# Three edits to a one-core twelve-stage network kernel: what is loaded first, where retention's angle tables are made, and when the convolution asks for the rows of its norm's scale

## The reference, cut to what matters

```python
def rmsnorm(x, gain=None):                 # in front of every mixer and MLP
    y = x * lax.rsqrt(jnp.mean(x * x, axis=-1, keepdims=True) + NORM_EPS)
    return y * gain

def rotary(t, positions):                  # in retention, on q and k
    half = t.shape[-1] // 2
    inv_freq = ROPE_BASE ** (-jnp.arange(half) / half)
    ang = positions[:, None, :, None] * inv_freq
    cos, sin = jnp.cos(ang), jnp.sin(ang)
    t1, t2 = t[..., :half], t[..., half:]
    return jnp.concatenate([t1 * cos - t2 * sin, t2 * cos + t1 * sin], axis=-1)

def conformer_conv(u, w_in, b_in, w_dw, ...):
    a, gate = jnp.split(u @ w_in + b_in, 2, axis=-1)
    h = a * jax.nn.sigmoid(gate)           # then 31 taps along the sequence
    ...
```

## Time and profile before

| | |
|---|---|
| median of 3 runs | 2310.38 us (2308.9 to 2310.8) |
| the profiled execution | 2314.51 us, of which 2312.7 us are the span from its first to its last instruction |
| PE busy | 2223.2 us, 96% of the span |
| PEld, DVE, ACT, POOL busy | 81%, 65%, 52%, 10% |
| moved by DMA | 368.93 MB, 160 GB/s on average |
| mean granted TensorE clock | 0.984 of full speed |

### The profile page before, as it was taken

One profiled execution on the slowest core, in us unless ns is written; L12 is line 12 of the kernel. 1 busy time (PEld: TensorE's weight loads), 2 busy tenths in 40 slices (PEclk: granted clock), 3 DMA queues, 4 the chain that ended last, 5 costly groups with the idle time before them and its releaser, 6 DMA issues.

```text
span 2312.7 us, 29470 instructions
## 1 busy us (share of the span) xinstructions
PE 2223.2 (96%) x11634; PEld 1880.1 (81%) x11634; DVE 1493.3 (65%) x2081; ACT 1197.6 (52%) x1817; POOL 223.6 (10%) x204
## 2 busy tenths in 40 slices
PE   6999999999999999999999999977999999999999
PEld 5877888887888878888878888766888888798887
DVE  4745755896656767557745665785665798454665
ACT  4555544755445745445555544654544666455543
POOL 0000100472000011000000100001000000152000
PEclk9999999999999999999999999988999999899999
DMA  6535566523665535554544655423655666302553
GB/s 214 182 129 181 168 196 193 162 68 97 191 197 174 166 107 187 195 198 156 182 145 146 194 184 195 167 92 90 197 183 181 199 170 184 127 1 88 186 189 121
DMA packets 201528, 368.93 MB, mean 160 GB/s; under 512 B 6943, under 2 KB 142495, under 8 KB 201392
## 3 DMA queue, kind: packets, MB, share of 16 engines
q1 hardware_dynamic: 197776, 358.70, 47.7%
q0 software_dynamic: 3616, 8.35, 2.2%
HBM read 365.97 MB, written 1.05 MB: 159 GB/s over the span
## 4 chain that ended last, share of the span: by engine, by line
PE 86%; DVE 6%; ACT 5%; issue 1%; POOL 1%; DMA 1%; SPq 0%; DVEq 0%; ACTq 0%
PE PS L656 46%; PE PS L781 14%; PE PS L778 6%; PE PS L765 6%; ACT whi L1311 2%; PE PS L934 2%; PE PS L1255 2%; DVE wlo L1854 2%; PE PS L1224 1%; PE PS L855 1%; PE PS L798 1%; ACT side L1361 1%; PE PS L1026 1%; ACT U L1346 1%; PE PS L780 1%
## 5 line engine op out<-in xcount | busy, mean ns | idle before, releaser
L1854 DVE TENSOR_TENSOR wlo<-raw,whi 128x1024 fp32r<-128x1024 f32 x658 | 792.4, 1229 | 206.2 <-ACT whi L1311 205.3
L1311 ACT ACTIVATE whi<-raw 128x1024 fp32r<-128x1024 f32 x680 | 700.1, 1056 | 392.4 <-PE PS L656 321.5
L781 PE MATMUL PS<-U,whi 128*128 128x512 f32 x1440 | 508.6, 397 | 5.1 <-DVE wlo L1854 5.1
L656 PE MATMUL PS<-whi,U 128*128 128x512 f32 x1728 | 483.2, 396 | 9.6 <-DVE U L2295 3.4
L656 PEld LDWEIGHTS PS<-whi,U 128*128 128x128 f32 x1728 | 322.5, 189 | 83.8 <-issue 14.3
L778 PE MATMUL PS<-U,wlo 128*128 128x256 f32 x1260 | 353.5, 281 | 0.0
L781 PEld LDWEIGHTS PS<-U,whi 128*128 128x128 f32 x1440 | 264.7, 188 | 58.5 <-issue 6.8
L656 PE MATMUL PS<-wlo,U 128*128 128x512 f32 x864 | 268.3, 392 | 0.0
L1980 DVE TENSOR_TENSOR AR<-PS,AR 128x512 f32<-128x512 f32 x96 | 66.3, 691 | 309.0 <-ACT AR L1398 308.9
L656 PE MATMUL PS<-whi,fH 128*128 128x512 f32 x832 | 258.1, 391 | 0.9 <-DVE fL L2103 0.9
L656 PE MATMUL PS<-whi,fL 128*128 128x512 f32 x832 | 256.4, 389 | 0.0
(11 more groups left out here) (323 smaller groups left out, 2451.0 us busy)
## 6 DMA issues: line engine op xcount, KB each, us to landing
raw<-in_mlp_w_up SPq DMA_DIRECT2D x64, 1024.0 KB, 5.6
raw<-in_mlp_w_down SPq DMA_DIRECT2D x64, 1024.0 KB, 5.0
raw<-in_ret_w_in SPq DMA_DIRECT2D x48, 1024.0 KB, 5.2
raw<-in_m_w_up SPq DMA_DIRECT2D x32, 1024.0 KB, 5.6
raw<-in_m_w_down SPq DMA_DIRECT2D x32, 1024.0 KB, 5.0
raw<-in_kv_w SPq DMA_DIRECT2D x24, 1024.0 KB, 5.2
raw<-in_ret_w_out SPq DMA_DIRECT2D x16, 1024.0 KB, 4.9
raw<-in_gla_w_in SPq DMA_DIRECT2D x12, 1024.0 KB, 5.1
```

The source lines that it names most:

```text
L656: mm = e.matmul(bank(b + nb), a, w[:, nb * 512:(nb + 1) * 512], start=(begins and n < 2), stop=(ends and n >= 4))
L781: mm = e.matmul(o, w_h[:, k, :], U[:, k, :, :, :], start=(k == 0), stop=(k == 7))
L1311: e.activation(split_half(whi, i, x), a, ACT.Copy).then_inc(HI.tick((i, x)), 1)
L1854: e.tensor_tensor(split_half(wlo, i, x), a, split_half(whi, i, x).bitcast(F32), ALU.subtract).then_inc(LO.tick((i, x)), 1)
```

## The change

1. **SP** issues the identity, half tt 0 of x, chunk 0 and half tt 1 of x, then waits until chunk 0 has landed, and issues chunks 1 to 3. **POOL** issues gT, `invf`, `positions` and decay, waits for the same landing, and then issues `relP`, `relN` and the two rows of norm gains.
2. **`angles`** becomes a generator. In RET0 DVE runs all of it behind the low part of chunk 0. For RET1 it runs in MLP2, two steps behind each of the parts f = 2, 3, ... of the MLP. **`sines`** runs in MLP2 behind part f = 11, with a `prime()` behind it, and in RET0 behind the squares of h. At the very start ACT runs a `prime()`, and it makes the high part of chunk 1 before that of tt 1 of u.
3. **In CONV** PE asks for the rows of the scale in the middle of the second chunk (between its two halves), ACT makes the high part of the third chunk before it copies the rows, and DVE makes its low part before `scaled(0)`.

```diff
             def gemm_b(i, b, free=(), mid=None):
                 for s in range(2):
+                    if s == 1 and mid is not None:
+                        mid()
                     e.wait_ge(*lo_cut(i, s))
...
-                rows_of_r(S, p.dg, 3)
                 for c in range(1, 8):
-                    gemm_b(c0 + c, 5 + (c - 1) % 3, free=[CXX[c - 3]] if c >= 4 else [])
+                    gemm_b(c0 + c, 5 + (c - 1) % 3, free=[CXX[c - 3]] if c >= 4 else [],
+                           mid=(lambda: rows_of_r(S, p.dg, 3)) if c == 1 else None)
...
             def act_mlp(S):
...
                     e.activation(fH[:, f % 3, :], m_x[f % 2], ACT.Copy).then_inc(FH.tick((S, f)), 1)
+                    if f == 11 and S + 1 in RETS:
+                        sines(S + 1)
+                        prime()
...
             def act_conv(S):
                 p, c0 = PC, first[S]
+                hi_of(c0 + 1, 1)
                 e.wait_ge(*ROWR[S])
...
             e.wait_ge(*s_gT[1])
+            prime()
             next_in(RET0, 0)
-            hi_to(1)
+            hi_to(2)
             next_in(RET0, 1)
-            hi_to(2)
             squares(RET0)
+            sines(RET0)
             act_ret(RET0)
...
             def dve_mlp(S):
...
+                steps = angles(S + 1) if S + 1 in RETS else iter(())
                 for f in range(16):
...
+                    if f >= 2:
+                        next(steps, None)
+                        next(steps, None)
...
             def dve_ret(S):
...
-                lo_of(c0, 1)
-                angles()
-                lo_of(c0 + 1, 1)
                 rows_of_r(S, p.dg)
-                lo_of(c0 + 2, 1)
+                lo_of(c0, 3)
                 tables()
...
             def dve_conv(S):
...
-                lo_of(c0, 1)
+                lo_of(c0, 2)
                 for c in range(8):
...
             lo_to(1)
+            for _ in angles(RET0):
+                pass
             u_lo_next(RET0 - 1, 1, 0, 1, 2, 3)
...
             def pool_ret(S):
...
-                load(p.relP, d["rel"][0].rearrange("(a p) n -> p a n", p=128), par["rel"])
-                load(p.relN, d["rel"][1].rearrange("(a p) n -> p a n", p=128), par["rel"])
                 load(p.invf, d["invf"], par["inv"])
                 load(p.posi, d["positions"][0, :].partition_broadcast(128), par["pos"])
                 load(p.lg, ...)
+                if S == RET0:
+                    e.wait_ge(*landed(0))
+                load(p.relP, d["rel"][0].rearrange("(a p) n -> p a n", p=128), par["rel"])
+                load(p.relN, d["rel"][1].rearrange("(a p) n -> p a n", p=128), par["rel"])
...
             load(gT[:, :, :], d["gains_in"], s_gT)
+            pool_ret(RET0)
             load_gain(RET0)
             load_gain(MLP0)
-            pool_ret(RET0)
...
             e.dma_start(ident[:, :], d["ident"]).then_inc(s_id.sem, 16)
-            for i in range(NCH):
+            load_x(0)
+            load_chunk(0)
+            load_x(1)
+
+            e.wait_ge(*landed(0))
+            for i in range(1, NCH):
                 load_chunk(i)
```

More of the change, by code:

```diff
@@ L752, in fresh_u, with gemm_b @@
                 return lambda k, tt: [UL[t, tt, k // (2 if t[1] == "in" else 4)]]
-            def gemm_b(i, b, free=()):
+            def gemm_b(i, b, free=(), mid=None):
                 for s in range(2):
+                    if s == 1 and mid is not None:
+                        mid()
                     e.wait_ge(*lo_cut(i, s))
@@ L1407, in act_mlp, with sines @@
                     seam(S)
+            def sines(S):
+                p = PR
+                for w, dst, arg in (("cos", p.cos, p.kf), ("sin", p.sin, p.ang)):
+                    e.wait_ge(*ANG[S, w])
+                    e.activation(dst, arg, ACT.Sin).then_inc(SIN.tick((S, w)), 1)
             def act_ret(S):
@@ L1422, in raw @@
                     ins.then_inc(QKCP.tick((S, n)), 1)
[L1424 to L1427, removed]
                 def log_decay():
@@ L1987, in dve_mlp, with angles @@
                     e.tensor_tensor(fL[:, f % 3, :], x, fH[:, f % 3, :].bitcast(F32), ALU.subtract).then_inc(FL.tick((S, f)), 1)
+                    if f >= 2:
+                        next(steps, None)
+                        next(steps, None)
                 lo_to(first[S + 1])
                 seam(S)
+            def angles(S):
+                p = PR
+                ang, kf = p.ang, p.kf
+                e.wait_ge(*s_ret_par["pos"][RETN[S]])
+                own(e.tensor_copy(ang, p.posi))
+                yield
+                settle()
+                e.wait_ge(*s_ret_par["inv"][RETN[S]])
+                own(e.tensor_scalar(ang, ang, p.invf[:, 0:1], None, ALU.mult))
+                yield
+                settle()
+                own(e.tensor_scalar(kf, ang, float(1 / (2 * np.pi)), 12582912.0, ALU.mult, ALU.add))
+                yield
+                settle()
+                own(e.tensor_scalar(kf, kf, -12582912.0, None, ALU.add))
+                c1 = 6.28125
+                c2 = float(np.float32(round((2 * np.pi - c1) * 2 ** 21) / 2 ** 21))
+                c3 = float(np.float32(2 * np.pi - c1 - c2))
+                for cc in (c1, c2, c3):
+                    yield
+                    settle()
+                    own(e.scalar_tensor_tensor(ang, kf, -cc, ang, ALU.mult, ALU.add))
+                yield
+                settle()
+                own(e.tensor_scalar(kf, ang, float(np.pi / 2), None, ALU.is_gt))
+                yield
+                settle()
+                own(e.scalar_tensor_tensor(kf, kf, float(-2 * np.pi), ang, ALU.mult, ALU.add))
+                yield
+                settle()
+                own(e.tensor_scalar(kf, kf, float(np.pi / 2), -3.1415925, ALU.add, ALU.max))
+                yield
+                settle()
+                e.tensor_scalar(kf, kf, 3.1415925, None, ALU.min).then_inc(ANG.tick((S, "cos")), 1)
+                e.tensor_scalar(ang, ang, 3.1415925, -3.1415925, ALU.min, ALU.max).then_inc(ANG.tick((S, "sin")), 1)
             def dve_ret(S):
                 p, c0 = PR, first[S]
-                lt, lg, ang, kf = p.lt, p.lg, p.ang, p.kf
+                lt, lg = p.lt, p.lg
                 cosb = p.cos.unsqueeze(1).to_broadcast([128, 2, 256])
```

28 lines of the change are left out of this document (1 added, 27 removed).

## The result

The changed kernel takes **2295.72 us** (median of 4 runs, 2295.4 to 2296.52) against 2310.2 of the kernel before on the same chip (4 runs, 2308.9 to 2310.8): ratio 0.9939, 95% interval 0.9921 to 0.9956. That is 14.5 us less; the forecast was 2294.1, 16.3 less, with a range of 2289.5 to 2301.0. The interval of the ratio stands for a gain of 10.2 to 18.3 us. The profiled execution took 2296.52 with a span of 2294.7; a second one, of the same kernel, is told of under the experiments.

A forecast was written before the change was run, and what follows sets the result against it. The prediction took PE, with 86% of the chain of waits, to bound the kernel. Start and RET0 12.3, RET1 4.2 and CONV -0.2 made 16.3 us, from 2310.38 to 2294.1 us; range 2289.5 to 2301.

The forecast's parts named there:

- Chunk 0 lands at 9.3; ACT's chain ends last, at 10.1: Start: ACT's high part of u, not chunk 0's landing, ends last; PE starts at 12.3 instead of 19.92.
- Chunk 1 lands at 17.6, 0.6 too late: Start: chunk 1, issued at 9.3, takes 8.3 us though needed by 17.0, so PE restarts at 21.0.
- The risk itself: Start: chunk 1 comes late, at 24.7, and PE restarts at 28.1; gain 6.8, time 2303.6, chance 0.15.
- Restart 7.0 earlier: Start: PE's restart with half tt 1 comes at 21.0 instead of 28.01, gaining 7.0 us.
- The wait of 3.8 and a dip of 1.5 go in RET0: RET0: PE's wait for the rows and the slow-clock stretch behind it vanish, 3.8 and 1.5 us.
- Rival B: RET0 and RET1: slow-clock dips do not go with the waits but fall elsewhere; gain 13.3, time 2297.1, chance 0.11.
- RET1: 2.7 + 1.5 = 4.2: RET1: the diagonal is made earlier, so PE's wait of 2.7 us goes with the dip that follows.
- The block in MLP2 costs nothing, cover 2.2: MLP2: ACT's added 3.6 us of loads, sines and prime stay hidden, with 2.2 us of cover left.
- Rival D: MLP2: ACT's block or DVE's steps reach PE, a 0.6 stall with a dip; 2.1 less, time 2296.2, chance 0.05.
- CONV -0.2: CONV: PE's 1.6 wait goes, but it idles 4.7 instead of 3.0 before the first sum; worth -0.2.
- rival E: CONV: more POOL products meet DVE's subtraction, each costing 1.9 us; with 20 more, 2332 us; chance 0.02.
- The sum: Whole kernel: 12.3 + 4.2 - 0.2 = 16.3 us off the median 2310.38, giving 2294.1 us.

The follow-up runs named there:

- best: Changed kernel with ten of PE's CONV taps before the first sum, x's second half after the wait for chunk 0, prime() before ACT's wait for gT: 2300.97 us.
- best_u_first: best with ACT making u of half tt 1 ahead of chunk 1's high part: 2293.64 us, ratio 0.9928.
- the second trace of before: Second profile of the kernel before, unchanged, taken in before_again; its profiled execution was 4.6 us shorter than the first.
- loads_only: Kernel before with only the new order of SP's and POOL's loads: 2303.68 us, ratio 0.9972.
- fill_wait: Kernel before with 22 unread PE products in front of the rows of the scale in both retentions: 2306.63 us, ratio 0.9987.
- double_block: Changed kernel with ACT's block in MLP2 made 3.0 us longer by two more table loads with one-column activations: 2295.32 us, ratio 0.9935.
- no_conv_edit: Changed kernel with the edit in the convolution undone: 2294.73 us, ratio 0.9932.
- the second set: Runs of after_again, no_conv_edit, best and no_pool_wait, beside which the kernel before took 2310.7 us.
- before_again: Kernel before, unchanged, profiled a second time: 2310.02 us, ratio 1.0001.
- after: Changed kernel, first measurement and trace, against the kernel before: 2295.72 us, ratio 0.9939.
- after_again: Changed kernel, unchanged, run and profiled a second time: 2296.43 us, ratio 0.9937.
- conv_fill: Changed kernel with eleven of PE's taps of group 7 put in front of the first sum in CONV: 2293.55 us, ratio 0.9932.
- no_pool_wait: Changed kernel in which POOL does not wait for chunk 0 before issuing rel: 2299.24 us, ratio 0.9949.
- best_pool_late: best with POOL's loads of rel and the gains waiting for chunk 1 instead of chunk 0: 2293.68 us, ratio 0.9928.

## Why the prediction was right, step by step

- **Chunk 0 lands at 9.3; ACT's chain ends last, at 10.1.** The landing was 1.2 late: 10.55, at the upper bound of 10.5 that I gave for "the rate no better" (2.3 MB in 10.5 us is 219 GB/s; the trace has 221). ACT's chain ended at 9.99, so it was the transfer that ended last after all, and PE started at 12.93 instead of 12.3. The step "That is no longer what ends last" was wrong; PE's start came 0.6 later than forecast.
- **Chunk 1 lands at 17.6, 0.6 too late.** It landed at 15.77, 5.2 us after its issue and not 8.3, and nobody waited. This offset the first miss, and PE took 7.8 us from its start to the restart instead of 8.1, because its pace changed sooner: restart at 20.76 for 21.0. That this agrees to 0.24 us is luck: three misses cancel. The 8.3 that I took, from a stretch in which one gain ran beside the chunk, was too long; 5.2 is the median of all 48 chunks of this kind on the page of the changed kernel. The risk itself was real: in best it landed at 19.75, and best loses 6.5 us of start against best_u_first.
- **Restart 7.0 earlier.** 7.3 and 7.7 against the trace that I worked from, 6.4 and 6.8 against the second trace of before; loads_only gives 7.1 and 6.2 by itself.
- **The wait of 3.8 and a dip of 1.5 go in RET0.** 5.5 for 5.3. fill_wait took away the dip alone: 1.5 in each retention. Rival B falls.
- **RET1: 2.7 + 1.5 = 4.2.** 4.4 in every comparison. The sizes are shown; which of DVE's two edits took the wait away is not.
- **The block in MLP2 costs nothing, cover 2.2.** Nothing was seen, and double_block measured the cover at 2.2. The Trainium skill, "ScalarE: Activation LUTs", What ACT_TABLE_LOAD costs, adds a drain to each switch; six loads in the two kernels (two in the changed kernel, four in double_block) show none: each takes 1.28 us, the next activation starts 0.01 to 0.02 behind it, and the trace decides. Rival D falls.
- **CONV -0.2.** This term was too kind by 0.3. PE idles 5.3 in front of the first sum where I said 4.7, because POOL's taps end 0.6 later (0 to 0.3 said); no_conv_edit puts the edit at -0.5. Their start is 0.1 later, inside what I allowed; the other 0.5 is rival E's mechanism, which I had left at nothing in the sum: one more product that meets DVE's subtraction in full. It was one product and not nine.
- **The sum.** The terms were 12.3, 4.2 and -0.2. The first traces say 12.6, 4.4 and 1.0, but the medians moved by 14.5 (14.3 for the second set) and not by 16.3. I can place only a part of the missing 1.8. The start's term was read from the latest of three traces with the old loads (restart at 28.01, 27.16 in before_again, 27.50 in fill_wait) and then taken off a median. That alone would make it too large by up to 0.85. But five traces with the changed start (after, after_again, double_block, no_conv_edit, conv_fill) restart at 20.76, 20.32, 20.30, 19.62 and 19.49, and the means differ by 7.5, more than my 7.0. CONV's term explains 0.3. DIFF and DIL, which the change doesn't touch, are together 1.6 to 1.7 us longer in the two traces of the changed kernel than in before_again, but only 0.3 to 0.4 longer than in the first trace of before; such differences come with stretches at half clock and stand between two traces of one kernel as well. And 16.3 lies inside the measured interval of 10.2 to 18.3: 25 runs of the kernel before went from 2307.4 to 2313.6. The mechanism is shown term by term; that the total agrees to 1.8 us is no better than this spread allows.

## What to carry to other kernels

When a span of transfers at the start bounds a kernel, hold back the other engine's queue first: here taking away POOL's wait cost 2.8 us of the median and 4 of the start, and SP's 0.9 and some 1, against after_again (the 0.9 is from two different sets of 4 runs and not clear of noise). Before an instruction that waits for a transfer is put in front of one on the path of PE, ask what the latter loses if the transfer is late; in best a chunk that landed 4.0 later than in the changed kernel cost 6.5 of the start, and putting u ahead of that chunk on ACT made it harmless. And take a second profile of the kernel before: a term read from one execution carries that execution's luck.

## What the runs showed of the chip

- A transfer's time is not given by its size: the same first chunk of 1 MB took 7.1 us in best (behind half of x, beside POOL's small loads), 8.9 in the changed kernel and 15.4 before; the next, issued when the first had landed, took 5.2 in the changed kernel, 7.7 in no_pool_wait, 7.0 in best_pool_late and 10.6 in best.
- At the start PE is slow though the clock column shows 1.00: 26 matmuls from 12.90 to 18.20, the starts of those from 13.31 to 17.58 being 0.213 us apart. In best, behind the wait of 5.1, the distance is the same 0.213 in a stretch shown at 0.51, and both turn to 0.12 later. The column has no record there: in all fourteen traces the first record of the clock falls where this first slow run of matmuls ends (14.4 us in best_u_first, 17.7 in the changed kernel, 25.2 before). By their distance the first matmuls run at half clock, and a 1.00 ahead of the first record should not be read.
- Idle time on PE costs more than itself: 1.5 us behind waits of 3.8 and 2.7, and in best 26 matmuls in 5.7 us (23.05 to 28.73) instead of 3.1, 2.6 behind a wait of 5.1. Behind the 1.6 in CONV a stretch of 3.4 us at 0.50 came in loads_only (from 427.2) and none in before.
- A product of POOL on 256 columns takes 0.93 us, and 2.83 in the six or seven places in CONV where it overlaps a low part of DVE by 2.2. Overlap alone doesn't tell the price: one that overlaps by 0.8 in the kernel before takes 0.93 all the same.
